# First shift tiles as one-column products, and the repeated row of c from products with the identity

## The chip, the cores and the metric

One core of one Trainium2 chip runs the whole program. The time is the device time of one execution in microseconds (us), and the number that is compared is the median over runs.

## The reference, cut to what matters

The program computes two deep blocks over 256 positions of width 1024. The change touches only what stands at the very beginning: the modulation of the first feed-forward layer.

```python
c_act = jax.nn.silu(c)                       # c: one row of 1024
mod = c_act @ w_ada[l] + b_ada[l]            # nine segments of 1024
sh1, sc1, g1, sh2, sc2, g2, sh3, sc3, g3 = jnp.split(mod, N_MOD, axis=-1)
x = x + 0.5 * g1 * swiglu(modulate(x, sh1, sc1), ffn1_gate[l], ffn1_up[l], ffn1_down[l])
...
modulate(x, shift, scale) = rms_norm(x) * (1 + scale) + shift
```

So before the first gate product there must be: silu of c, the scale and the shift of layer 0 (each 1024 values from a 1024 x 1024 piece of `w_ada`), and the root mean square of x at each position.

## The kernel before, in words

Everything is held with the 1024 features on 128 partitions in 8 tiles (k = 0 to 7) and the 256 positions along the free axis. Weights come through a ring of 8 slots (`ring`) of 512 KB each, filled by one queue (SP, sync) in the order in which TensorE's program takes them; slot n + 8 waits until chunk n has been used. The other start loads (vectors, constants, x) go over the ACT queue.

A weight chunk has one of three kinds. A "cut" chunk is split by ScalarE (`weight_upper`, L2459) and VectorE (`weight_lower`, L1736) into two halves in fp32r; a product then runs as one pass of 512 columns with the upper and one of 256 with the lower half. An "ada" chunk is used by VectorE alone: L1747 multiplies 128 rows of transposed `w_ada` by `c_rows` (the row silu(c), repeated on all partitions) and sums along the row, which gives one tile (128 values) of the modulation. A "whole" chunk is used by TensorE in plain fp32.

In layer 0 the eight scale tiles and the first four shift tiles (`BY_ROW = 4`) are "ada" chunks. The other four shift tiles come from TensorE: `shift_rows` multiplies the column c (as a weight of one column) with 512 moving columns of `w_ada_row`, two products for each of four chunks; ScalarE copies the resulting row of 512 values to SBUF (L2534), `shift_columns` turns it back into four columns with four products, and VectorE adds the bias (L1788).

TensorE's order at the start is: `hold` (products of the identity with itself into an unused bank, which only fill time), then row chunk 0, the sums of squares of x (`squares_sum`, 16 products with one moving column), `spread` (two products that spread the reciprocal root over partitions), row chunks 1 to 3, `shift_columns`, `hold`, and the first gate tile. VectorE's `normalise` makes for each k the scaled x (L1799) and, after ScalarE has rounded the sum with the shift (`normed_upper`, L2539), the lower half (`normed_lower`, L1807); in between it does the ada chunks that are due. The first gate tile takes k after k as `normed_lower` comes in; everything behind it on TensorE follows without waits.

All products are recorded at one line (L601), so the rows below are told apart by their tiles and shapes. In plain fp32 one product is two records.

Of the kernel before, what the change touches and what calls it, by code (L numbers as in the profile page):

```python
# [12 lines left out]
P = 128  # L13
# [43 lines left out]
BY_ROW = 4  # L57
SHIFTS_AT = 5
ADA_AHEAD = 6
ROW_W = D - BY_ROW * P  # L60
ROW_CHUNKS = KD * ROW_W // CW
ROW_BANK = 8 - ROW_W // 512
LAG = 2
# [94 lines left out]
SHARED = {"root_part": "root", "c_silu": "c_act", "shift_row": "c_act", "shifts": "ada_mod",  # L158
# [77 lines left out]
def program(nc, dram, out, seen, stream):  # L236

    ctx = ExitStack()
    with ctx:
# [231 lines left out]

        def pair_bank(f):
            return (0, 1, 2, 3, 6, 7)[f % 6]
# [46 lines left out]
        ADA_FIRST = [seg * KD + k for k in range(KD) for seg in (1, 0) if seg or k < BY_ROW]  # L520
# [3 lines left out]
        first_row = work[0:1, 0:ROW_W].rearrange("p (b c) -> p b c", c=512)  # L524
# [25 lines left out]
        def _(pe):  # L550
# [14 lines left out]
            def cut(name, i, which="weight_lower"):  # L565

                n = take_chunk(name, i, CW, "cut")
                j = split_no[n] = len(split_no)
                pe.wait_ge(*of(which, j))
                return (w_hi[:, j % SPLITS, :], w_lo[:, n % RING, :]), ("cut_used", j), ("weights_used", n)  # L570

# [223 lines left out]
            def shift_rows(j):  # L795

                w, used = arrived("w_ada_row", j)
                if j == 0:
                    refill(6, 7)
                passes = CW // 512  # L800
                for m in range(passes):
                    i, b = (j, ROW_BANK + m) if ROW_W == D else (passes * j + m, ROW_BANK)
                    mn = mm(bank[0:1, b, :], vec("c", i), w[:, m * 512:(m + 1) * 512], i == 0, i == KD - 1)
                mn.then_inc(*did("shift_row_raw", j, also=[used]))
                readers[6] = readers[7] = [("shift_row", 0)]

            def shift_columns():

                pe.wait_ge(*of("shift_row", 0))
                refill(3)  # L810
                for k in range(BY_ROW, KD):
                    a = (k - BY_ROW) * P
                    mn = mm(bank[:, 3, k:k + 1], work[0:1, a:a + P], ones[0:1, 0:1], True, True)
                mn.then_inc(*did("shift_cols_raw", 0))
                readers[3] = [("shifts", 0)]
# [2404 lines left out]
```

## Time and profile before

| what | value |
| --- | --- |
| median of 3 runs (lowest, highest) | 2163.93 us (2163.75, 2165.28) |
| time of the profiled execution | 2162.36 us |
| span of the profiled execution | 2160.6 us |
| PE busy | 2103.5 us (97%) |
| DVE busy | 1521.8 us (70%) |
| ACT busy | 1167.8 us (54%) |
| first feed-forward product starts | 39.99 us |
| its 16th record (the end of the first gate tile) hands over at | 43.23 us |

The span runs from the first to the last instruction, and the execution's own time is 1.8 us more. PE is TensorE, DVE VectorE, ACT ScalarE, POOL GpSimd, SP the sync engine, whose queue loads the weights. Busy time counts records that overlap once.

### The profile page before, as it was taken

The page shows a single profiled execution, that of the slowest core. Times are in us where ns is not written, and L with a number is a line of the kernel's source. Part 1 is how long each engine was busy: PE and PEld are TensorE (multiplying, and loading weights), DVE is VectorE, ACT ScalarE, POOL GpSimd, SP SyncE. Part 2 cuts the span into 40 slices and gives each one's busy share as a digit, 9 for nine tenths or more (in the row PEclk, how much of TensorE's full clock was granted, in tenths as well). Part 3 has the DMA queues.
Part 4 walks back from the last instruction along what each step waited for, and adds up shares of the span by engine and source line. Part 5 has one row for each costly group of instructions (what it writes and reads, how often), then busy time and mean ns, then how long its engine had stood idle before and what let it go on. Part 6 is the DMA issues. An engine that isn't in the chain of part 4 may idle for free.

```text
span 2160.6 us, 40536 instructions
## 1 busy us (share of the span) xinstructions
PE 2103.5 (97%) x16664; PEld 1888.2 (87%) x16664; DVE 1521.8 (70%) x2114; ACT 1167.8 (54%) x2030; POOL 374.2 (17%) x357
## 2 busy tenths in 40 slices
PE   8999999999999999999999999999999988999998
PEld 5888988988888889899888998988888877898887
DVE  6897757788779878577776687477558544647754
ACT  4564556665546545576655575465446632446542
POOL 0131021211102110221011002120132640123001
PEclk9999999999999999999999999999999999999999
DMA  8987772567668777725565544345543400434552
GB/s 306 352 302 271 271 253 99 176 237 265 251 217 303 292 257 270 251 94 181 211 216 205 195 168 155 135 172 192 180 163 136 166 4 4 149 129 162 189 185 98
DMA packets 116679, 424.66 MB, mean 197 GB/s; under 512 B 12944, under 2 KB 14736, under 8 KB 115600
## 3 DMA queue, kind: packets, MB, share of 16 engines
q1 hardware_dynamic: 112896, 409.52, 53.7%
q10 hardware_dynamic: 3600, 12.55, 1.6%
q8 instruction: 133, 2.18, 0.4%
q14 instruction: 50, 0.41, 0.1%
HBM read 418.35 MB, written 3.67 MB: 195 GB/s over the span
## 4 chain that ended last, share of the span: by engine, by line
PE 82%; DVE 7%; issue 5%; ACT 4%; POOL 1%; DMA 1%; SPq 0%; POOLq 0%; ACTq 0%; DVEq 0%
PE banks L601 81%; DVE weight_lower L1736 2%; POOL heap L3030 1%; ACT weight_upper L2459 1%; ACT xn_t L2637 1%; DMA weight_ring<-w_ada_row_dram 0%; PE banks L1556 0%; ACT heap L2637 0%; PE banks L1135 0%; DMA weight_ring<-w_in_dram 0%; DVE nmax L1883 0%; DVE heap L2076 0%; ACT heap L2651 0%; DVE xn_t L1954 0%; DVE xn_t L1957 0%
## 5 line engine op out<-in xcount | busy, mean ns | idle before, releaser
L1736 DVE TENSOR_TENSOR weight_lower<-weight_ring,weight_upper 128x1024 fp32r<-128x1024 f32 x580 | 743.2, 1288 | 265.9 <-ACT weight_upper L2459 263.9
L601 PE MATMUL banks<-xn_halves,weight_upper 128*128 128x512 f32 (+1 forms) x3680 | 808.3, 342 | 0.9 <-DVE xn_halves L2059 0.7
L2459 ACT ACTIVATE weight_upper<-weight_ring 128x1024 fp32r<-128x1024 f32 x580 | 608.4, 1054 | 299.9 <-PE banks L601 195.0
L601 PEld LDWEIGHTS banks<-xn_halves,weight_upper 128*128 128x128 f32 x3680 | 611.9, 188 | 67.7 <-issue 1.4
L601 PE MATMUL banks<-xn_halves,weight_lower 128*128 128x256 f32 x2832 | 519.4, 281 | 2.8 <-DVE weight_lower L1736 1.6
L601 PEld LDWEIGHTS banks<-xn_halves,weight_lower 128*128 128x128 f32 x2832 | 431.6, 188 | 30.0 <-DVE weight_lower L1736 2.4
L601 PE MATMUL banks<-hidden,weight_upper 128*128 128x512 f32 x1216 | 308.8, 393 | 0.6 <-DVE heap L2201 0.6
L3030 POOL TENSOR_TENSOR heap<-heap 128x256 f32<-128x256 f32 x120 | 121.7, 1018 | 873.8 <-ACT heap L2754 587.5
L601 PEld LDWEIGHTS banks<-hidden,weight_upper 128*128 128x128 f32 x1216 | 217.0, 189 | 37.7 <-DVE heap L2201 0.7
L1747 DVE CUSTOM_DVE_ANT_0 weight_ring<-weight_ring,c_rows,vecs 128x1024 f32<-128x1024 f32 x140 | 184.4, 1321 | 19.3 <-DMA weight_ring<-w_ada_dram 18.8
L601 PEld LDWEIGHTS banks<-hidden,weight_lower 128*128 128x128 f32 x1216 | 169.2, 190 | 14.0
L601 PE MATMUL banks<-hidden,weight_lower 128*128 128x256 f32 x1216 | 173.2, 282 | 0.0
L3017 POOL TENSOR_TENSOR heap<-heap 128x256 f32<-128x256 f32 x88 | 76.4, 869 | 479.9 <-ACT heap L2569 479.4
L601 PE MATMUL banks<-heap 64*64 64x64 f32 (+8 forms) x2432 | 120.0, 256 | 16.5 <-issue 5.5
L601 PEld LDWEIGHTS banks<-heap 64*64 64x64 f32 (+4 forms) x2432 | 102.8, 144 | 31.4 <-issue 20.8
L601 PE MATMUL banks<-heap,weight_ring 64*64 64x15 f32 (+2 forms) x944 | 107.0, 287 | 0.8 <-DVE heap L2230 0.4
L2560 ACT ACTIVATE heap<-banks 128x512 f32<-128x512 f32 x88 | 52.2, 593 | 94.2 <-PE banks L601 94.2
L601 PEld LDWEIGHTS banks<-heap,weight_ring 64*64 64x64 f32 (+2 forms) x944 | 86.2, 158 | 15.2 <-issue 2.7
L1829 DVE TENSOR_TENSOR heap<-banks,heap 128x512 f32<-128x512 f32 x88 | 60.4, 686 | 30.7 <-ACT heap L2560 30.5
L601 PE MATMUL banks<-weight_ring,heap 128*128 128x128 f32 (+1 forms) x528 | 73.4, 289 | 0.0
L601 PEld LDWEIGHTS banks<-weight_ring,heap 128*128 128x128 f32 x528 | 63.7, 192 | 6.4 <-issue 6.3
L2486 ACT ACTIVATE heap<-x_t 128x256 f32<-128x256 f32 x56 | 22.4, 411 | 84.0 <-DVE x_t L1821 79.4
(311 smaller groups left out, 2415.5 us busy)
## 6 DMA issues: line engine op xcount, KB each, us to landing
weight_ring<-w_ada_dram SPq DMA_DIRECT2D x140, 512.0 KB, 4.6
weight_ring<-ffn_gate_dram SPq DMA_DIRECT2D x88, 512.0 KB, 3.9
weight_ring<-ffn_up_dram SPq DMA_DIRECT2D x88, 512.0 KB, 4.5
weight_ring<-ffn_down_dram SPq DMA_DIRECT2D x88, 512.0 KB, 3.4
weight_ring<-m_w_up_dram SPq DMA_DIRECT2D x64, 512.0 KB, 3.2
weight_ring<-m_w_down_dram SPq DMA_DIRECT2D x64, 512.0 KB, 3.2
weight_ring<-w_in_dram SPq DMA_DIRECT2D x58, 512.0 KB, 4.3
weight_ring<-b_w_rkv_dram SPq DMA_DIRECT2D x24, 512.0 KB, 3.6
```

The costliest lines, as they stand in the source:

```text
L601: return nc.tensor.matmul(o, w, r, start=first, stop=last)
L1736: V.tensor_tensor(w_lo[:, n % RING, :], ring[:, n % RING, :], w_hi[:, j % SPLITS, :].bitcast(F32), ALU.subtract).then_inc(*did("weight_low ...
L1747: V.tensor_tensor_reduce(w, w, c_rows[:, :], half, vec("b_ada", i), ALU.mult, ALU.add, mod[:, i:i + 1]).then_inc(*did("ada_mod", i, also=[ ...
L1829: V.tensor_tensor(gu[:, f % 4], bank[:, b:b + 2, 0:S], gu[:, f % 4], ALU.add).then_inc(*did("gate_up", (s, f)))
L2459: A.activation(w_hi[:, j % SPLITS, :], ring[:, n % RING, :], ACT.Copy).then_inc(*did("weight_upper", j))
L2486: A.activation(sq[:, k, :], X[:, k, :], ACT.Square).then_inc(*did("squares", (n, k)))
L2560: A.activation(gu[:, f % 4], bank[:, b:b + 2, S:2 * S], ACT.Copy).then_inc(*did("gate_up_half", (s, f)))
L2637: A.activation(s_, s_, ACT.Exp, bias=nmax[:, u % 4, j:j + 1], accum_out=den[:, u % 4, j:j + 1]).then_inc(*did("exp", (l, u, j), also=[("ex ...
L3017: G.tensor_tensor(gu[:, f % 4, 0, :], gu[:, f % 4, 0, :], gu[:, f % 4, 1, :], ALU.mult).then_inc(*did("hidden", (s, f)))
L3030: G.tensor_tensor(acc, acc, sum_tile(n, what, f), ALU.add).then_inc(*did("sum_added", (n, what, f)))
```

## The change

It does four things.

1. All eight shift tiles of layer 0 come from TensorE. `first_shift(k)` takes a chunk of `w_ada_shift` (the 1024 x 128 columns of tile k, as eight 128 x 128 blocks), uses the eight blocks as weights and the eight columns of c as one moving column each, and sums in one column of a bank. ScalarE adds the bias in `shift` (new L2541). `shift_rows`, `shift_columns` and the four shift chunks on VectorE go away.
2. `c_rows` is no longer loaded (512 KB). The column form of c (4 KB) and the identity (64 KB) are loaded first on SP's queue, eight products of a column of c, repeated 128 times, with the identity make the repeated row in two banks, and ScalarE's silu reads it from there.
3. The small work on `lam` (two exponential-type functions on ScalarE, four small operations on VectorE) stands before the squares of x, where it stood behind the root.
4. The first gate tile is split: k = 0 to 4, then `first_shift(7)`, then k = 5 to 7. VectorE's lower halves run two tiles behind the scaling for this layer (`lag`), and its weight half for the gate comes at k = 6 (`FIRST_SPLIT`). `hold` is 4 products after the products of c and 2 after each of the first six shift tiles; the `hold` of 20 before the gate tile is gone.

```diff
-        ADA_FIRST = [seg * KD + k for k in range(KD) for seg in (1, 0) if seg or k < BY_ROW]
+        ADA_FIRST = [KD + k for k in range(KD)]
...
-            sp.dma_start(c_rows[:, :], dram["c_rows"]).then_inc(*did("c_rows_in", 0, by=16))
+            sp.dma_start(vec("c", 0, KD), dram["c_columns"]).then_inc(*did("c_in", 0, by=16))
+            sp.dma_start(ident, dram["ident"]).then_inc(*did("ident_in", 0, by=16))
...
-            def shift_rows(j):
-            def shift_columns():
+            def first_shift(k):
+
+                w, used = arrived("w_ada_shift", k)
+                b = shift_bank(k)
+                refill(b)
+                for j in range(KD):
+                    mn = mm(bank[:, b, 0:1], w[:, j * P:(j + 1) * P], vec("c", j), j == 0, j == KD - 1)
+                mn.then_inc(*did("shift_raw", k, also=[used]))
+                readers[b] = [("shifts", k)]
...
-                    project_wide_first(items(0)[0:1], xn_hl, ("normed_lower", norm), ADA_FIRST[-1:])
+                    name, i, done, readers_of, b = items(0)[0]
+                    refill(b)
+                    w, *used = cut_taken(name, i)
+                    held["first_cut"] = len(order)
+                    first_shift(KD - 2)
+                    ada_take(ADA_FIRST[-1:])
+                    pe.wait_ge(*of("weight_lower", 0))
+                    took = w, used, done, readers_of, b
+                    first_tile(took, xn_hl, norm, range(FIRST_SPLIT - 1))
+                    first_shift(KD - 1)
+                    first_tile(took, xn_hl, norm, range(FIRST_SPLIT - 1, KD))
...
+            for k in range(KD):
+                mn = mm(cols(k // 4, P, k % 4 * P), vec("c", k).broadcast_to((P, P)), ident, True, True)
+            mn.then_inc(*did("c_raw", 0))
+            readers[0] = readers[1] = [("c_act", 0)]
+            hold(2, 4)
             pe.wait_ge(*of("consts_in", 0))
             pe.wait_ge(*of("c_silu", 0))
-            hold(2, 8)
-            for k in range(BY_ROW):
-                ada_take(ADA_FIRST[2 * k:2 * k + 2])
+            ada_take(ADA_FIRST[0:1])
+            for k in range(KD - 2):
+                ada_take(ADA_FIRST[k + 1:k + 2])
+                first_shift(k)
+                hold(2, 2)
                 if k == 1:
                     for j in range(KD):
                         squares_sum(0, j, KD)
+                elif k == 2:
                     spread(0)
-                elif k > 1:
-                    hold(2, 4)
-                shift_rows(k)
-            ada_take(ADA_FIRST[2 * BY_ROW:-1])
-            shift_columns()
-            hold(2, 20)
...
+                    if n == 0:
+                        if k == FIRST_SPLIT:
+                            work_ahead(held["first_cut"])
+                        act.wait_ge(*due("shift_raw", k))
+                        A.activation(mods(0, 0, k), bank[:, shift_bank(k), 0:1], ACT.Identity, bias=vec("b_ada", k)).then_inc(
+                            *did("shifts", k))
+                        act.wait_ge(*due("shifts", k))
                     act.wait_ge(*due("scaled", (n, k)))
```

TensorE's program before, from behind the spread to the first gate record. `1x512` is a product of one weight column with 512 moving columns, `consts` alone is a `hold`, `consts,heap` with `128x1` is here `shift_columns`:

```order
L601 MATMUL banks<-weight_ring,vecs 1x512 [waits weights_in_5]
L601 MATMUL banks<-weight_ring,vecs 1x512
L601 MATMUL banks<-consts 128x128 x4
L601 MATMUL banks<-weight_ring,vecs 1x512 [waits weights_in_0]
L601 MATMUL banks<-weight_ring,vecs 1x512
L601 MATMUL banks<-consts 128x128 x4
L601 MATMUL banks<-weight_ring,vecs 1x512 [waits weights_in_3]
L601 MATMUL banks<-weight_ring,vecs 1x512
L601 MATMUL banks<-consts,heap 128x1 [waits c_act]
L601 MATMUL banks<-consts,heap 128x1 x3
L601 MATMUL banks<-consts 128x128 x20
L601 MATMUL banks<-xn_halves,weight_upper 128x512 [waits normed_lower,weight_lower]
```

The same stretch in the changed program. The first row of a shift tile waits for its chunk, and the row `x7` holds its other seven products:

```order
L605 MATMUL banks<-vecs,weight_ring 128x1 [waits shifts,weights_in_0]
L605 MATMUL banks<-vecs,weight_ring 128x1 x7
L605 MATMUL banks<-consts 128x128 x2
L605 MATMUL banks<-vecs,weight_ring 128x1 [waits shifts,weights_in_2]
L605 MATMUL banks<-vecs,weight_ring 128x1 x7
L605 MATMUL banks<-consts 128x128 x2
L605 MATMUL banks<-vecs,weight_ring 128x1 [waits shifts,weights_in_4]
L605 MATMUL banks<-vecs,weight_ring 128x1 x7
L605 MATMUL banks<-consts 128x128 x2
L605 MATMUL banks<-vecs,weight_ring 128x1 [waits shifts,weights_in_6,c_act]
L605 MATMUL banks<-vecs,weight_ring 128x1 x7
L605 MATMUL banks<-xn_halves,weight_upper 128x512 [waits normed_lower,weight_lower]
```

Where there were three pairs of 512-column products, four small ones and 28 holds, there are now four shift tiles of eight one-column products each (k = 3 to 6), with three holds of two between them. The tile k = 7 follows inside the gate tile. Tiles 0 and 1 stand in front of the sums of squares and tile 2 between them and the spread, each with a hold of two.

ScalarE's program before, from the root to the weight half of the gate (`xn_t,mod` is the upper half of one tile of x, `heap<-banks 1x512` the copy of the row):

```order
L2493 ACTIVATE root<-banks,consts 128x2 [waits bank_filled]
L2716 ACT_TABLE_LOAD
L2716 ACTIVATE lam<-lam 128x8 [waits dve_chain]
L2718 ACT_TABLE_LOAD
L2718 ACTIVATE lam<-lam 128x8 [waits lam_exp]
L2539 ACTIVATE xn_halves<-xn_t,mod 128x256 [waits scaled] x4
L2534 ACTIVATE heap<-banks 1x512 [waits bank_filled]
L2539 ACTIVATE xn_halves<-xn_t,mod 128x256 [waits scaled,ada_mod]
L2539 ACTIVATE xn_halves<-xn_t,mod 128x256 [waits scaled]
L2459 ACTIVATE weight_upper<-weight_ring 128x1024 [waits weights_in_7]
```

In the changed program the end of the same stretch reads (`banks,vecs 128x1` is the bias of one shift tile):

```order
L2541 ACTIVATE mod<-banks,vecs 128x1 [waits bank_filled]
L2545 ACTIVATE xn_halves<-xn_t,mod 128x256 [waits scaled,shifts]
L2541 ACTIVATE mod<-banks,vecs 128x1 [waits bank_filled]
L2545 ACTIVATE xn_halves<-xn_t,mod 128x256 [waits scaled,shifts]
L2541 ACTIVATE mod<-banks,vecs 128x1 [waits bank_filled]
L2545 ACTIVATE xn_halves<-xn_t,mod 128x256 [waits scaled,shifts]
L2464 ACTIVATE weight_upper<-weight_ring 128x1024 [waits weights_in_5]
```

The pair stands six times ahead of the weight half of the gate. Each upper half now waits for its own shift tile from TensorE, and the weight half of the gate stands behind the sixth of them. The two rows of `lam` have moved ahead of the squares of x.

## Rows read from the trace of the kernel before

**Rows 1.** The page: the chain that ended last, by engine.

```profile
PE 82%; DVE 7%; issue 5%; ACT 4%; POOL 1%; DMA 1%; SPq 0%; POOLq 0%; ACTq 0%; DVEq 0%
```

**Rows 2.** Chain that ended last, 0 to 90 us: start, us, what.

```profile
12.39 10.50 PE banks L601 x36
...
42.77 47.46 PE banks L601 x266
```

**Rows 3.** PE in order of time: start, us, what, xrecords, [idle before <-releaser].

```profile
7.51 3.78 PE L601 MATMUL banks<-consts 128*128 128x128 f32 x16 [7.51 <-DMA consts<-consts_dram]
12.39 3.57 PE L601 MATMUL banks<-weight_ring,vecs 128*1 128x512 f32 x4 [1.10 <-DMA weight_ring<-w_ada_row_dram]
15.89 6.99 PE L601 MATMUL banks<-consts,heap 128*128 128x1 f32 x32
23.59 1.20 PE L601 MATMUL banks<-consts,root 128*128 128x128 f32 x4 [0.71 <-DVE root L1783]
24.72 3.12 PE L601 MATMUL banks<-weight_ring,vecs 128*1 128x512 f32 x4
...
31.76 1.88 PE L601 MATMUL banks<-weight_ring,vecs 128*1 128x512 f32 x4
...
35.29 4.73 PE L601 MATMUL banks<-consts 128*128 128x128 f32 x40
...
40.80 0.39 PE L601 MATMUL banks<-xn_halves,weight_upper 128*128 128x512 f32 x1
...
41.15 0.39 PE L601 MATMUL banks<-xn_halves,weight_upper 128*128 128x512 f32 x1
...
43.23 2.09 PE L601 MATMUL banks<-xn_halves,weight_upper 128*128 128x512 f32 x8
```

**Rows 4.** ACT in order of time.

```profile
5.51 1.06 ACT L2709 ACTIVATE c_rows<-c_rows 128x1024 f32<-128x1024 f32 x1 [2.08 <-DMA c_rows<-c_rows_dram]
...
11.26 2.56 ACT L2486 ACTIVATE heap<-x_t 128x256 f32<-128x256 f32 x8 [4.60 <-DMA x_t<-x_dram]
...
23.20 1.28 ACT L2716 ACT_TABLE_LOAD   x1
...
26.01 0.21 ACT L2718 ACTIVATE lam<-lam 128x8 f32<-128x8 f32 x1
...
36.41 1.04 ACT L2459 ACTIVATE weight_upper<-weight_ring 128x1024 fp32r<-128x1024 f32 x1
38.44 0.51 ACT L2539 ACTIVATE xn_halves<-xn_t,mod 128x256 fp32r<-128x256 f32 x1 [0.99 <-DVE xn_t L1799]
```

**Rows 5.** DVE in order of time.

```profile
24.83 0.87 DVE L1799 SCALAR_TENSOR_TENSOR xn_t<-x_t,mod,banks 128x256 f32<-128x256 f32 x2 [0.84 <-PE banks L601]
...
33.41 1.28 DVE L1747 CUSTOM_DVE_ANT_0 weight_ring<-weight_ring,c_rows,vecs 128x1024 f32<-128x1024 f32 x1
...
38.72 1.22 DVE L1736 TENSOR_TENSOR weight_lower<-weight_ring,weight_upper 128x1024 fp32r<-128x1024 f32 x1
```

**Rows 6.** Windows of all engines: at the end PEclk, DMA share, GB/s.

```profile
10.00:15.00 5.00, 3.90 (x11) 1.34 (x9) 2.53 (x4) 3.72 (x9) 0.00 (x0) 1.00 1.03 415
```

**Rows 7.** PE in order of time, one-column products at 164 us.

```profile
164.01 0.95 PE L601 MATMUL banks<-consts,heap 128*128 128x1 f32 x8
```

**Rows 8.** PE in order of time, around 1658 us.

```profile
1655.80 1.84 PE L601 MATMUL banks<-consts,heap 128*128 128x2 f32 x16
...
1658.35 0.28 PE L601 MATMUL banks<-shifted_lower,weight_upper 128*128 128x256 f32 x1
...
1659.25 0.41 PE L601 MATMUL banks<-shifted_lower,weight_upper 128*128 128x256 f32 x1
```

**Rows 9.** Windows of PE there: us, busy (xrecords), PEclk, DMA share, GB/s.

```profile
1658.00:1659.00 1.00, 1.00 (x9) 0.91 0.65 262
1659.00:1660.00 1.00, 1.00 (x7) 0.50 0.00 0
...
1662.00:1663.00 1.00, 1.00 (x10) 0.88 0.00 0
```

More of the change, by code:

```diff
@@ L157 @@
 FILLED = ("square_sums", "rstd", "head_sums", "head_spread", "chunk_used")
-SHARED = {"root_part": "root", "c_silu": "c_act", "shift_row": "c_act", "shifts": "ada_mod",
+SHARED = {"root_part": "root", "c_silu": "c_act",
           "x_last": "x_first",
@@ L793, in project_wide, with first_tile, project_wide_first @@
                 readers[b] = readers_of
-            def shift_rows(j):
[L797 to L805, printed above, removed]
-            def shift_columns():
[L809 to L815, printed above, removed]
-            def project_wide_first(items, x, ready, after=()):
+            def first_shift(k):
[6 more added lines that the diff above has]
+                readers[b] = [("shifts", k)]
+            def first_tile(took, x, norm, ks):
+                w, used, done, readers_of, b = took
+                for k in ks:
+                    pe.wait_ge(*of("normed_lower", (norm, k)))
+                    mm_upper(b, w, k, x, k, k == 0)
+                    mn = mm_lower(b, w, k, x, k, k == KD - 1)
+                    if k == KD - 1:
+                        mn.then_inc(*did(*done, also=used))
+                        readers[b] = readers_of
+            def project_wide_first(items, x, ready):
                 for *_, b in items:
@@ L821, in project_wide_first @@
                 took = [(*cut(name, i), done, readers_of, b) for name, i, done, readers_of, b in items]
-                held.setdefault("first_cut", len(order))
-                ada_take(after)
                 for k in range(KD):
@@ L2718, in _ @@
             A.activation(lam[:, 2, :], lam[:, 2, :], ACT.Ln, bias=1.0).then_inc(*did("lam_ln", 0))
+            act.wait_ge(*due("x_in", 0))
+            squares(0, None)
+            root_of(0)
             for l in range(DEPTH):
@@ L3140, in laid_out @@
     d = {}
-    d["c_rows"] = np.broadcast_to(a["c"][0], (P, D))
+    d["c_columns"] = columns(a["c"].reshape(-1))
+    d["ident"] = CONSTS["ident"]
     d["x"] = a["x"][0].T.reshape(KD, P, S).transpose(1, 0, 2)
-    d["consts"] = np.concatenate([CONSTS[k] for k in CONSTS if k not in ATTN + DELTA], 1)
+    d["consts"] = np.concatenate([CONSTS[k] for k in CONSTS if k not in ATTN + DELTA + ["ident"]], 1)
     d["delta_consts"] = np.concatenate([CONSTS[k] for k in DELTA], 1)
```

80 lines of the change are left out of this document (33 added, 47 removed).

## Prediction

> **What bounds the kernel now.** I read the page first: TensorE is 82% of the chain that ended last [rows 1], so what is gained or lost at the start is kept to the end. The chain over the first 90 us [rows 2] shows where the start ends: TensorE is on it from 12.39, when the first row chunk has landed, then there is a relay with VectorE and ScalarE, and from 42.77 on TensorE alone for 47 us. The mark that counts is therefore the end of the first gate tile, where TensorE goes on with the next chunk: 43.23 [rows 3].
>
> Then I read TensorE in order of time for its pace. At 7.51, 16 records of the identity with itself take 3.78 us, 236 ns each; at 35.29 the same form takes 4.73 us for 40, 118 ns each [rows 3]. The first is 1.2 GHz, the second 2.4 GHz. The PEclk column says 1.00 even where the pace is the slow one [rows 6], so at the start of the trace it must be read from durations. The four 512-column records take 3.57 us at 12.39, 3.12 us at 24.72 and 1.88 us at 31.76: the clock rises at the last of the four at 24.72, near 27.2, after 3.6 us of wide products without a break. The 32 one-column records at 15.89 take 6.99 us, 218 ns each: TensorE issued them without a gap for 7 us, and the clock did not rise.
>
> The opposite case stands later. Eight one-column records at 164.01 take 0.95 us, 119 ns each [rows 7]: that is their price at the high clock. But at 1655.80, 16 narrow records (two columns) take 1.84 us, and 1.2 us later, in the middle of dense products, the clock falls: 256-column records go from 0.28 to 0.41 us [rows 8], and PEclk, which does show this one, is 0.50 in between: its means of 0.91 and 0.88 at the edges put the fall at 1658.8 and the rise at 1662.2 [rows 9]. The records at 1658.35 and 1659.25 stand on either side. Less than 2 us of narrow products among wide ones were enough to lose the clock.
>
> **The change part by part.** A shift tile is 8 products, so 16 records. Its cost is bounded by 16 x 119 ns = 1.9 us [rows 7] and 16 x 218 ns = 3.5 us [rows 3]. A hold of two is 4 records: 0.47 us or 0.94 us. In the new order a hold of two is the only wide work between shift tiles, while around 1655.80 there were full trains of wide products on both sides and the clock still fell. I take the slow price for all eight: the slow row is the nearer one, since it too has nothing wide around it.
>
> The Trainium skill (TensorE: Matmul & The Clock Gate, Part 1 and "Loop structure matters more than you think") explains the low clock by idleness and says that matmuls kept back to back stay warm. By that rule the eight tiles would run at 1.9 us each, which is the first rival below. The trace disagrees twice: 7 us of gapless one-column records without a rise, and a fall after gapless narrow ones.
>
> The start: c and the identity are 68 KB in place of 512 KB, and 68 KB of constants move off the ACT queue. The first shift chunk is third in the ring like the first row chunk, which was in use at 12.39 [rows 3]; 512 KB fewer (both queues) at 415 GB/s [rows 6] are 1.3 us: 11.1 us. The products for c begin at about 3.6 us, between 3.0 (the fastest a small load could be there) and 5.5 (when the 512 KB had landed [rows 4]); 16 records are 3.8 us, silu 1.06, so silu(c) is ready near 8.6 and hidden under the load. The two functions of `lam` are now ahead of the squares on ScalarE, 3.0 us with their table loads (23.20 to 26.22 [rows 4]): 8.6 + 3.0 = 11.6, so the squares end at 14.2 instead of 13.8. Hidden too: TensorE does not reach them before 20. The price of `lam` would be 0.4 us if the cover were gone. On VectorE four chunks of 1.3 us [rows 5] go away, of which two were behind the root: 2.7 us less. That is hidden now, because VectorE will wait for TensorE.
>
> TensorE's own queue from 11.1 us, at the low clock:
>
> - shift 0, hold, shift 1, hold: 2 x (3.5 + 0.94) = 8.9, to 20.0
> - sums of squares, unchanged 7.0: to 27.0
> - shift 2 and hold 4.4, spread 1.2: to 32.6. The root (0.5 us on ScalarE and VectorE) is hidden under shift 2
> - shifts 3, 4, 5 with holds: 13.3, to 45.9
> - shift 6: 3.5, to 49.4
> - gate tile k = 0 to 4: 0.35 us each at the high clock (40.80 to 41.15 [rows 3]), 0.70 at half of it: 3.5, to 52.9
> - shift 7: 3.5, to 56.4
> - gate tile k = 5 to 7: 2.1, to 58.5
>
> Is anything else later? VectorE starts at 32.6 instead of 24.8. The weight half of the gate stands on ScalarE behind the upper half of k = 5, thus behind shift 5 (45.0): 0.2 + 0.5 + 1.04 [rows 4], then 1.2 on VectorE [rows 5]: 47.9, under shift 6. The chunk of shift 6 can be loaded only once shift 2 is done (30.5), 15 us ahead of its use. Behind shift 7 ScalarE and VectorE need 0.2 + 0.5 + 0.5 = 1.2 us, to 57.6, while k = 5 and 6 last until 57.8. So TensorE is the bound throughout: 58.5 against 43.23, 15.3 us late.
>
> Before, the high clock was there at 43.23; now it is still to rise. Dense work begins at 56.4. The row of 1658.8 shows 3.4 us at 1.2 GHz under dense work, and at the start 8.4 us (7.51 to 15.89) with one gap of 1.1 us did not bring the rise. Thus it comes between 59.8 and 64.8; what lies behind 58.5 costs half its length: 0.7 to 3.1 us. I take 1.3, near the short end, because at 24.72 it also took 3.6. In the other direction, the products for c and the hold are 5.7 us of wide work and may lift the clock for the first shift tile: 0 to 1.6 us back, I take 0.5.
>
> Sum: 15.3 + 1.3 - 0.5 = 16.1 us. The profiled execution had 2162.36 us, 1.8 over its span; with the sum 2178.5. The median of the runs is 1.6 higher, 2163.93, so the forecast is 2180.0 us, 0.74% slower. Later stages give nothing back, TensorE is full there.
>
> **The rivals.**
>
> *One-column products run at the high clock* (the other sign). For it: 164.01, and the holds put between. Then shift 0 and 1 end with holds at 16.0, the squares at 19.9, shift 2 and hold 22.3, spread 22.8, against 24.8 before. From there VectorE is the bound: 16 operations at 0.40 (two take 0.87 with their overlap), 4 chunks at 1.33 (1.28 and a read), one weight half 1.2 [rows 5] are 12.9 us, with 1.6 us of waiting for shift 7 about 37.3, the tile ends at 37.7: 5.5 us earlier, 2158.4. It decides if the clock rises before the first shift tile and stays; against it stand the two stretches named.
>
> *The clock is held until the squares and falls there.* The 5.7 us of wide work lift it, holds keep it over two shift tiles, the 16 narrow products in a row lose it. Squares end at 19.9, then the slow queue: shift 2, hold, spread 5.6, three tiles with holds 13.3, shift 6, five gate steps, shift 7, three gate steps 12.6, the end at 51.4; 8.2 + 1.3 = 9.5 later, 2173.4.
>
> *The clock rises and falls several times*, lifted by a hold and lost in the next tile: the time lies between those two, 2159 to 2173. Against it: even 3.8 us of wide records at 7.51 did not raise it [rows 3].
>
> *A load is late*, as the ring gives a slot back only after a slow shift tile. The slots have 15 us of slack; at most 1 to 2 us on top.
>
> **How the numbers follow.** Low clock throughout 0.86, clock until the squares 0.05, high clock 0.05, up and down 0.04. The range must reach over the unknowns of the likeliest case: 2.4 us of the rise, 1.6 us of the lift at the start, 0.5 us of loads on either side, and the next rival: 2173 to 2184. A measurement of this kernel tells 0.2% (4.3 us) from no change. Faster by more than that is only most of the second case, 0.05; within 0.2%: 0.04; slower: 0.91.
>
> **What would show it.** Right: one-column records of the shift tiles at about 218 ns, spread near 32 us, the gate tile split around a shift tile of 3.5 us, the second gate chunk begun near 58 us, VectorE waiting for TensorE several us in all between 30 and 50, and 256-column records still at 0.4 us for a few us after 58. Wrong: one-column records at 119 ns, or a first gate record before 40. A first shift tile much later than 11 us would move everything by as much, and mean that the load of 512 KB was not what the start waited for.

## The result and the profile after

| kernel | median | lowest to highest | runs |
| --- | --- | --- | --- |
| before | 2164.61 us | 2163.75 to 2168.66 | 4 |
| changed | 2189.44 us | 2188.07 to 2190.70 | 4 |

The ratio is 1.0111, with a 95% interval of 1.0097 to 1.0124: the change makes the kernel 24.8 us slower. The forecast was slower too, but 2180.0 us with a range of 2173 to 2184; the time lies 9.4 us above the forecast and 5.4 us above the range. The profiled execution of the changed kernel took 2188.07 us (span 2186.2 us), 25.7 us more than that of before. PE is busy 2129.2 us (97%).

Its chain that ended last, first by engine from the page, then the view of 0 to 110 us (start, us, what), against [rows 1, 2]:

```profile
PE 83%; DVE 6%; issue 4%; ACT 4%; POOL 1%; DMA 1%; SPq 0%; POOLq 0%; ACTq 0%; DVEq 0%
```

```profile
2.58 10.26 DMA weight_ring<-w_ada_shift_dram
12.84 0.14 issue
12.98 97.13 PE banks L605 x484
```

From 12.98 on there is TensorE alone. No relay with the other engines is left, so TensorE's pace at the start is paid in full. TensorE in order of time, against [rows 3]:

```profile
4.41 3.65 PE L605 MATMUL banks<-consts,vecs 128*128 128x128 f32 x16 [4.41 <-DMA consts<-ident_dram]
7.90 1.06 PE L605 MATMUL banks<-consts 128*128 128x128 f32 x8
12.98 3.54 PE L605 MATMUL banks<-vecs,weight_ring 128*128 128x1 f32 x16 [4.02 <-DMA weight_ring<-w_ada_shift_dram]
16.38 1.20 PE L605 MATMUL banks<-consts 128*128 128x128 f32 x4
17.38 3.41 PE L605 MATMUL banks<-vecs,weight_ring 128*128 128x1 f32 x16
...
21.64 6.83 PE L605 MATMUL banks<-consts,heap 128*128 128x1 f32 x32
...
33.59 3.41 PE L605 MATMUL banks<-vecs,weight_ring 128*128 128x1 f32 x16
...
49.66 0.77 PE L605 MATMUL banks<-xn_halves,weight_upper 128*128 128x512 f32 x1
...
53.01 3.41 PE L605 MATMUL banks<-vecs,weight_ring 128*128 128x1 f32 x16
...
58.63 3.62 PE L605 MATMUL banks<-xn_halves,weight_upper 128*128 128x512 f32 x8
```

The eight hold records at 7.90 take 132 ns each, so the clock had just risen. Every one-column tile behind the idle time of 4.02 us takes 3.41 to 3.55 us for 16 records, the slow price. The first gate tile ends at 58.63, against 43.23 before. The clock column shows the fall and the rise (windows of PE: us, busy, PEclk, DMA share, GB/s):

```profile
11.00:12.00 1.00, 0.00 (x0) 0.62 1.03 422
12.00:13.00 1.00, 0.02 (x1) 0.50 1.02 418
61.00:62.00 1.00, 1.00 (x3) 0.50 0.95 385
62.00:63.00 1.00, 1.00 (x8) 0.78 0.93 373
```

The 1.2 GHz level thus lasts from 11.2 to 62.4 us. That is the forecast's mechanism, but it does not explain the whole loss. To find the rest I compare the starts of one kind of instruction, ScalarE's loads of function tables, of which each trace has 35 in the same order. The table gives, in us, how much later than in the profiled execution of before five of them start, for all kernels of this document (worked out from the traces). Where a stretch of low clock is named below, it is read from PEclk in windows of 1 us, and its length is twice the sum of what is missing to 1.00.

```
mark (its start before)          5th 52.53  7th 279.65  9th 302.77  33rd 1836.09  35th 1962.57
changed                            +17.1      +18.7       +22.7       +25.0         +25.7
changed, second profile            +16.6      +17.8       +22.0       +25.2         +25.2
before, second profile              -1.8       -0.4        +0.0        +3.5          +3.8
e1  shift tiles 128 wide            -2.8       -1.5        +3.5        +9.0          +9.7
e2  c's row by identity alone       -3.6       -2.1        -1.0        +5.7          +5.9
e3  no holds                        +7.5       +8.7        +8.6       +15.3         +15.3
e4  e1 and sums 128 wide            -4.4       -4.1        +2.8        +7.5          +8.3
e5  longer hold                    +11.3      +12.1       +11.6       +15.4         +16.2
e6  before, 40 more holds           +8.7       +8.4       +12.4       +17.8         +18.3
e7  e4 without holds                -6.6       -6.9        -7.5        -8.5          -8.4
e8  before, sums 128 wide           -2.8       -2.7        -2.4        +1.0          +1.2
e9  e1 without holds                -0.8       +2.4        +2.0        +4.2          +4.3
e10 shift tiles alone              +16.5      +17.7       +24.4       +27.6         +27.8
```

The changed kernel loses 17.1 us at the start (16.1 were forecast), 1.6 by the 7th mark, 4.0 between the 7th and the 9th, and 3.0 behind it. So there were two questions for the chip: is the low clock made by the one column, and what are the later 8.6 us?

### The profile page after: what moved, and what is told of

Read it like the earlier page. It is cut to its first block, busy times and chain, and to the rows that moved or that the text cites. A ratio compares the mean times of both kernels' runs of the same rounds, so it can differ in the third digit from the quotient of the medians.

```text
span 2186.2 us, 40704 instructions
## 1 busy us (share of the span) xinstructions
PE 2129.2 (97%) x16744; PEld 1920.8 (88%) x16744; DVE 1512.1 (69%) x2105; ACT 1168.7 (53%) x2037; POOL 371.9 (17%) x357
## 4 chain that ended last, share of the span: by engine, by line
PE 83%; DVE 6%; issue 4%; ACT 4%; POOL 1%; DMA 1%; SPq 0%; POOLq 0%; ACTq 0%; DVEq 0%
PE banks L605 82%; DVE weight_lower L1749 1%; POOL heap L3037 1%; ACT weight_upper L2464 1%; ACT xn_t L2643 1%; DMA weight_ring<-w_ada_shift_dram 0%; PE banks L1569 0%; ACT heap L2643 0%; PE banks L1144 0%; DVE nmax L1888 0%; ACT heap L2657 0%; DVE heap L2081 0%; DVE xn_t L1959 0%; ACT spare L2961 0%; DVE xn_t L1962 0%
## 5 line engine op out<-in xcount | busy, mean ns | idle before, releaser
L1760 DVE CUSTOM_DVE_ANT_0 weight_ring<-weight_ring,c_rows,vecs 128x1024 f32<-128x1024 f32 x136 | 176.4, 1301 | 22.5 <-DMA weight_ring<-w_ada_dram 21.8
L605 PE MATMUL banks<-heap,weight_ring 64*64 64x15 f32 (+2 forms) x944 | 112.9, 294 | 3.1 <-issue 2.6
```

The lines of the kernel that those rows point to most:

```text
L605: return nc.tensor.matmul(o, w, r, start=first, stop=last)
L1760: V.tensor_tensor_reduce(w, w, c_rows[:, :], half, vec("b_ada", i), ALU.mult, ALU.add, mod[:, i:i + 1]).then_inc(*did("ada_mod", i, also=[ ...
```

## The experiments

All medians of before in this part come from the same chip as the kernel beside them. A product in plain fp32 is two records; a `hold(2, n)` is n products, so 2n records.

**Width and holds.** Experiment e1 makes the shift tiles 128 columns wide (c's column repeated; the same sum stands in each column). Experiment e3 takes away the holds between the tiles.

```diff
 e1
-  mn = mm(bank[:, b, 0:1], w[:, j * P:(j + 1) * P], vec("c", j), j == 0, j == KD - 1)
+  mn = mm(bank[:, b, 0:P], w[:, j * P:(j + 1) * P], vec("c", j).broadcast_to((P, P)), j == 0, j == KD - 1)
 e3
   first_shift(k)
-  hold(2, 2)
```

> The changed kernel, but each product of a shift tile moves the column of c repeated 128 times in place of one column: the same number of products and weight loads, 128 times the moving columns; the reader takes column 0. Theory (narrow products lose TensorE's clock): the clock comes up during the first two tiles, a tile costs 1.9 us in place of 3.4, the first gate tile ends near 42 us in place of 58.6 and needs no new rise, so 15 to 19 us less than the changed kernel: 2170 to 2174 us. Rival (the cost is the number of products, each bound by its weight load, and the clock has other reasons): no gain, or up to 2 us slower (236 in place of 218 ns a record), 2189 to 2192 us.

> The changed kernel without the six holds of two between the shift tiles. Theory (the clock is low there in any case): the holds are pure cost, 6 x 0.95 us = 5.7 us less than the changed kernel, 2183 to 2184.5 us, and the records of shift tiles stay at 213 to 218 ns. Rival (the holds help the clock): no gain, or slower.

Measured: e1 2172.56 us against 2166.85, ratio 1.0035 (1.002 to 1.005); e3 2177.20 us, ratio 1.0055 (1.0038 to 1.0072). First TensorE of e1 in order of time, then e3's:

```profile
10.93 2.02 PE L605 MATMUL banks<-vecs,weight_ring 128*128 128x128 f32 x16 [1.62 <-DMA weight_ring<-w_ada_shift_dram]
...
15.73 3.94 PE L605 MATMUL banks<-consts,heap 128*128 128x1 f32 x32
19.52 3.76 PE L605 MATMUL banks<-vecs,weight_ring 128*128 128x128 f32 x16
...
27.47 1.95 PE L605 MATMUL banks<-vecs,weight_ring 128*128 128x128 f32 x16
```

```profile
10.87 6.30 PE L605 MATMUL banks<-vecs,weight_ring 128*128 128x1 f32 x32 [1.77 <-DMA weight_ring<-w_ada_shift_dram]
17.03 6.96 PE L605 MATMUL banks<-consts,heap 128*128 128x1 f32 x32
...
28.26 13.65 PE L605 MATMUL banks<-vecs,weight_ring 128*128 128x1 f32 x64
41.78 0.77 PE L605 MATMUL banks<-xn_halves,weight_upper 128*128 128x512 f32 x1
...
45.12 2.14 PE L605 MATMUL banks<-vecs,weight_ring 128*128 128x1 f32 x16
```

In both the first chunk came early, behind an idle time of under 2 us. The wide tile then costs 1.95 to 2.05 us at the high clock, the narrow one 3.2 to 3.5 us. A wide record costs 122 ns at the high clock and a narrow one 119 [rows 7]: with its stationary operand changed for each product, the 128 columns are nearly free. At the start of e1 only the sums, still one column wide, lose the clock (it is low from 18.9 to 25.7 us, so the tile at 19.52 is wide and slow). In e3 the clock falls at 11.6 us within the first tile and stays low: 80 one-column records stand there in a row without a gap and, behind the spread, another 64. It is back at 45.7, after the five gate steps at 41.78, and low once more from 49.2 to 52.6. e3 is 12.2 us faster than the changed kernel, twice the 5.7 us that were expected: the start gives 9.6 us of it (the six holds are 24 records of about 250 ns, 6 us, and the clock is back by 46 instead of 62), and a piece of 4 us at the 9th mark is missing, which is taken up below.

e9, described further down, is e3 with 128 columns in the shift tiles and no other difference. Its first two tiles and its tiles 3 to 6:

```profile
11.11 5.44 PE L605 MATMUL banks<-vecs,weight_ring 128*128 128x128 f32 x32 [1.87 <-DMA weight_ring<-w_ada_shift_dram]
...
25.24 7.51 PE L605 MATMUL banks<-vecs,weight_ring 128*128 128x128 f32 x64
```

Its clock falls at 12.0 us within the first tile too, but the wide tiles bring it back at 15.4 and, after the sums, at 25.7. It is low for 13.7 us before 40 us, and e3's for 34.1, and the first gate tile ends at 42.39 instead of 49.19.

**Hold the clock through the wait.** Experiment e5 fills the idle time ahead of the first shift tile in the changed kernel.

```diff
-            hold(2, 4)
+            hold(2, 16)
             pe.wait_ge(*of("consts_in", 0))
```

> The changed kernel with 16 instead of 4 rounds of two hold products behind the products of c, so that TensorE has work in most of the 4.0 us for which it waited for w_ada_shift before the first shift tile; nothing else is altered. Theory: the clock fell in that kernel at 11.2 us, in this idle time, but the one-column products behind it are not enough to keep it, so it falls again within the shift tiles and squares: the first gate tile still ends later than 50 us (58.6 us in the changed kernel), and the time is 2180 to 2190 us. The rival says that a clock that is high on entry stays high through the one-column products, as the narrow products of 7.8 to 11.2 us had it: then the squares' two blocks of 32 take 3.8 us instead of 6.9, the shift tiles 1.9 instead of 3.5, the first gate tile ends near 42 us and the time is 2170 us or less. For the later pause: with 24 more instructions ahead of it, the pause of 2.6 us with the reason issue at about 307 us, in the stage of 64x15 products, is gone or stands elsewhere by the theory that their number places it, and is unchanged by the rival that the waits of data set it.

Measured: 2182.23 us against 2166.04, ratio 1.0068 (1.0053 to 1.0083), 7.2 us under the changed kernel. TensorE in order of time:

```profile
7.99 4.00 PE L605 MATMUL banks<-consts 128*128 128x128 f32 x32
11.83 1.92 PE L605 MATMUL banks<-vecs,weight_ring 128*128 128x1 f32 x16
13.61 0.69 PE L605 MATMUL banks<-consts 128*128 128x128 f32 x4
14.29 2.63 PE L605 MATMUL banks<-vecs,weight_ring 128*128 128x1 f32 x16
16.79 1.20 PE L605 MATMUL banks<-consts 128*128 128x128 f32 x4
17.78 6.83 PE L605 MATMUL banks<-consts,heap 128*128 128x1 f32 x32
```

This case leaves idle time out. The clock is high on entry, there is no gap, and it falls at 15.4 us, inside the second one-column tile. (The rival in the expectation calls the work of 7.8 to 11.2 us narrow; it was eight hold records of 128 columns and then idle time.) So the idle time of 4.02 us only brings the fall forward; without it the one-column work makes it. The forecast's lift for the first tile (0.5 us, at most 1.6) exists here and not in the changed kernel, whose clock fell while it waited. The pause that is dealt with below is gone too.

**One half at a time.** Experiment e2 is the kernel before with c's row made by products with the identity (part 2 of the change alone, with its shorter hold). Experiment e10 is the changed kernel with the 512 KB load and the hold of 8 back (the shift tiles, with parts 3 and 4 of the change).

```diff
 e2, e10 the other way round
-  sp.dma_start(c_rows[:, :], dram["c_rows"]).then_inc(*did("c_rows_in", 0, by=16))
+  sp.dma_start(vec("c", 0, KD), dram["c_columns"]).then_inc(*did("c_in", 0, by=16))
+  sp.dma_start(ident, dram["ident"]).then_inc(*did("ident_in", 0, by=16))
...
+  for k in range(KD):
+      mn = mm(cols(k // 4, P, k % 4 * P), vec("c", k).broadcast_to((P, P)), ident, True, True)
```

> The kernel before with only the second part of the change: c and the identity are loaded (68 KB), eight products make the repeated row, and the shift stays with the 512-column products. If the 512 KB load is what the start waits for, the first row chunk is used 1.3 us earlier and the time is about 1 us less than before. If the start is bound by what is behind it (TensorE's squares at the low clock, then VectorE), or the small loads are no earlier, the difference is under 0.5 us. If the products for c and the hold behind them bring the clock up early, the sums of squares run at 119 in place of 218 ns and up to 3 us are gained.

> The changed kernel with c's repeated row loaded as 512 KB again, as in the kernel before, so that only the one-column shift tiles remain of the change (its other half alone was measured at 2166.5 us, ratio 1.0003). Theory: the loss is the shift tiles' and this kernel has all of it: the clock stays low from the start until the gate tiles, which begin when their tiles are split, so the first gate tile ends between 57 and 62 us and the time is 2184 to 2194 us. If the loss came from both halves together, by the idle time that the early products leave ahead of the first shift tile, this kernel ends well under 2184 us.

Measured: e2 2166.49 us against 2166.85, ratio 1.0003 (0.9993 to 1.0012); e10 2188.05 us against 2165.55, ratio 1.0098 (1.0080 to 1.0116). So part 2 costs nothing that is clear of noise, and the loss lies in the rest. Parts 3 and 4 have no run of their own, but e1, which keeps both and only widens the shift tiles, is 2.8 us ahead of before at the 5th mark: at the start the loss is that of the one-column tiles. In e2 the first row chunk is in use at 11.06 instead of 12.39 [rows 3], 1.3 us earlier as worked out, and by the 5th mark its profiled execution is 1.8 us ahead even of the second profile of before, but the measured time does not show it. e10's first shift tile starts at 12.88 and its gate tile ends at 58.55, within 0.1 us of the changed kernel. Its clock column must not be read there: it shows 1.00 at 20 us, where the 16 records at 17.30 take 3.41 us. As in [rows 6], it stands at 1.00 until the first step that the trace has.

**The pause near 290 us.** Between the 7th and the 9th mark the changed kernel loses 4.0 us. The cause in its trace is a pause of TensorE that ends with "issue": it waited for no data. Here are that row of the changed kernel and its clock (windows of PE):

```profile
307.58 3.86 PE L605 MATMUL banks<-heap,weight_ring 64*64 64x15 f32 x18 [2.62 <-issue]
```

```profile
307.00:308.00 1.00, 0.41 (x11) 1.00 0.09 37
308.00:309.00 1.00, 1.00 (x3) 0.60 0.06 25
309.00:310.00 1.00, 1.00 (x4) 0.50 0.07 20
311.00:312.00 1.00, 1.00 (x4) 0.69 0.00 0
```

The pause is 2.62 us, and behind it the clock is low for 3.4 us. The kernel before has 0.34 us in this stage, 63 records ahead of its end (the last eight are 128x256 products with the same tiles):

```profile
285.93 2.93 PE L601 MATMUL banks<-heap,weight_ring 64*64 64x15 f32 x63 [0.34 <-issue]
```

e1 and e4 have the long pause too, at the same 18 records before the end of the stage, though their start is fast; e3 has none. What these share is the number of TensorE's records: 16664 before, 16744 in the changed kernel, e1 and e4, 16720 in e3. Hence experiment e6, the kernel before with 40 hold products, 80 records, more and nothing else (its expectation calls the records products and places them ahead of the products of c, while they stand ahead of the first gate tile), and a second profile of each of the two kernels.

```diff
-            hold(2, 20)
+            hold(2, 60)
```

> The kernel before with 60 instead of 20 rounds of two hold products ahead of the first product of c, 80 products of TensorE more and no other edit: the products of c and all that follows start later. At the low clock 80 products of two columns add at most 8.5 us (106 ns each), of which what the load of c's row already takes is hidden. Theory: the number of instructions ahead also places a pause in the stage of 64x15 products; it is 0.34 us in before and 2.6 to 3.6 us in three kernels whose start has more instructions, and a stretch of low clock stands beside it. Then this kernel loses, beyond what its first gate tile ends later, 2 to 4 us between 280 and 303 us. The rival, that this pause is made by what the change does to the data, expects nothing there: the loss at 303 us equals the loss at 53 us within 0.5 us.

> The kernel before, unchanged, profiled once more. If the low-clock stretches after 60 us belong to the program, this trace has the same single one as the profiled execution of before (1658 to 1663 us, 3.4 us at the low clock) and a span within 0.5 us of its 2160.6. If they vary from execution to execution, the low stretches stand at other places or in another number and the span is several microseconds away (the plain runs of before reach from 2160.3 to 2169.8). In both cases the pause of TensorE in the stage of 64x15 products near 290 us that ends with the reason issue stays 0.34 us, since the program is the same; if that pause moves or grows here too, its cause is not the number of instructions ahead of it.

> The changed kernel, unchanged, profiled once more. If the pause of 2.6 us with the reason issue at about 307 us belongs to the program, it is here again at the same place, between 2 and 4 us long; if it comes from one execution it is gone. The 51 us at the low clock at the start should be the same within 2 us, and the first gate tile end at 58 to 59 us. The later low stretches should stand partly elsewhere, as in the two traces of the kernel before; the time 2186 to 2192 us.

Measured: e6 2177.50 us against 2166.04, ratio 1.0049 (1.0034 to 1.0064); b1 2166.16 us; b2 2187.58 us. The row of e6, then that of b1, then that of b2, then e10's (TensorE in order of time):

```profile
297.45 3.75 PE L601 MATMUL banks<-heap,weight_ring 64*64 64x15 f32 x15 [2.75 <-issue]
```

```profile
285.97 2.92 PE L601 MATMUL banks<-heap,weight_ring 64*64 64x15 f32 x63 [0.73 <-issue]
```

```profile
306.87 3.74 PE L605 MATMUL banks<-heap,weight_ring 64*64 64x15 f32 x18 [2.83 <-issue]
```

```profile
308.69 3.99 PE L604 MATMUL banks<-heap,weight_ring 64*64 64x15 f32 x9 [2.92 <-issue]
```

e6 has nothing of the change and has the pause: it loses 8.7 us by the start and 3.9 us more between the 7th and the 9th mark. Counting TensorE's records from the start to the pause gives 1974 in the changed kernel, b2, e1 and e4, 1977 in e6 and 1975 in e10. The pause is tied to a place in TensorE's own instruction stream, in six traces among the short 64x15 products.

The same shows late in the program, where short 64x64 products stand. All fourteen traces have such a wait at record 13068 to 13073 (0.45 to 1.89 us) and again at 13320 to 13324 (0.73 to 1.63 us), although up to 104 records more stand ahead of it in one kernel than in another. The second of the two in before and in e5 (TensorE in order of time):

```profile
1781.11 0.57 PE L601 MATMUL banks<-heap 64*64 64x64 f32 x23 [1.33 <-issue]
```

```profile
1790.85 1.40 PE L605 MATMUL banks<-spare,heap 64*64 64x64 f32 x65 [1.63 <-issue]
```

What TensorE waits for can be read from the DMA queues. The page of the changed kernel has one of the kind "instruction" (packets, MB, share):

```profile
q8 instruction: 134, 2.20, 0.4%
```

Its packets are 16 KB each. There are 133 for the 16664 records of before and 134 for the 16744 of the changed kernel, one for about 125 records, and the places above are 125 (1849 and 1974) or 251 records apart. The table has the packet next to the pause, in us (worked out from the packets in the traces):

```
                 record  TensorE stops  packet            TensorE goes on
changed          1974    304.96         305.39 to 306.36  307.58
changed, second  1974    304.04         304.62 to 305.51  306.87
e1               1974    284.79         286.17 to 287.05  288.42
e4               1974    282.12         282.58 to 283.50  284.93
e6               1977    294.71         295.02 to 296.03  297.45
e10              1975    305.76         306.25 to 307.25  308.69
before           1849    285.59         283.59 to 284.51  285.93
before, second   1849    285.23         283.58 to 284.59  285.97
e8               1849    282.93         281.35 to 282.36  283.57
e5               1974    no stop        295.43 to 296.39  (record at 297.79)
```

TensorE goes on 1.2 to 1.4 us behind the end of a packet each time. It is so everywhere: the fourteen traces have 71 waits of at least 0.8 us that end with "issue", and each ends 1.2 to 1.7 us behind the end of such a packet, though one comes only every 16 us in the mean. By these times TensorE waits there for the next 16 KB of its own instructions. In the six long pauses the packet starts only after TensorE has stopped; in before and e8 it starts 1.6 to 2.0 us ahead of the stop. In e5, with 104 records more than before, it ended 1.4 us before the record was due, and nothing waits. In e3, e7 and e9, with 56 records more, record 1974 lies behind the stage, in 128x512 products, and in before, e2 and e8 in 128x256 products, and the packet is there in time. What makes the packet start late in six traces is not shown.

**The rest, and the way to a faster kernel.** Experiment e4 is e1 with the sums of squares 128 columns wide as well (each column holds the same sum; one sum of the joined norms stays at one column); e7 is e4 without the holds between the tiles; e9 is e1 without them, its sums narrow; e8 is the kernel before with only the sums wide.

```diff
 e4, e7, e8 (and the later sums alike)
-  mn = mm(bank[:, 4 + t, 0:1], src[:, k, t * P:(t + 1) * P], ones[:, 0:1],
+  mn = mm(bank[:, 4 + t, 0:P], src[:, k, t * P:(t + 1) * P], ones[:, 0:P],
```

> The first experiment, and in addition every sum of squares in the program (start, norms of all layers, the memory, the latents) moves 128 columns of ones in place of one. Theory: the clock no longer falls at the start once it is up, and the later falls that stand beside sums of squares (at 277 us in the trace of the changed kernel) go away: the gate tile ends near 39 us and the time is 2156 to 2164 us, below the kernel before. Falls beside the narrow products that are left (15 columns wide near 308 and 895 us, 64 x 64 tiles near 1840 us) can stay. Rival for the later 8.6 us (not the clock, but loads that come late because the ring is shifted): the later part keeps its extra time, whatever the sums look like.

> The kernel with products of 128 columns in the shift tiles and in all sums of squares, without the hold products between the shift tiles. Theory: the wide products keep the high clock by themselves, so leaving out the holds costs nothing and takes away their own time (two rounds after each shift tile); the first gate tile ends at 37.5 to 38.8 us (38.8 with the holds), the pause near 290 us is gone as in the narrow kernel without holds, and the time is 2164 to 2169 us, 3 to 5 us under the same kernel with the holds. If the holds keep the clock, it falls between the shift tiles here: low stretches before 40 us, the first gate tile past 42 us, and 2172 us or more.

> The kernel before with 128 columns instead of one in all sums of squares, the widening that the fastest kernel so far also has; nothing of the change. It tells what of that kernel's 2161.2 us the widening alone gives. Theory: the sums at 15.9 us take 3.8 us at the high clock instead of 6.99 at the low one if the clock is high by then, as in the second trace of the kernel before, and the clock does not fall beside them: the first gate tile ends 1 to 4 us earlier and the time is 2161 to 2165 us, so most of what was gained belongs to the widening. The rival, that the early load of c is what gains, has this kernel at 2165 to 2168 us, as before.

> The changed kernel with 128 columns in the shift tiles and no hold products between them, but one column in the sums of squares as it was. Theory: the shift tiles ahead run at the high clock, the 32 narrow sums lose it again, and a stretch of 5 to 9 us at the low clock follows before the later wide tiles bring it back, as it did with the holds (18 to 26 us there); the first gate tile ends at 38 to 41 us and, without the pause near 290 us, the time is 2164 to 2169 us, 3 to 6 us over the kernel that has wide sums too. If the time is 2161 to 2163, the width of the sums was worth nothing.

Measured, each against before on its chip: e4 2171.15 us, ratio 1.0034 (1.0022 to 1.0046); e7 2161.24 us, 0.9976 (0.9964 to 0.9989); e8 2164.52 us, 0.9993 (0.9982 to 1.0004); e9 2166.51 us, 0.9993 (0.9981 to 1.0006). e4 misses its forecast of 2156 to 2164 us, e7 is faster than its 2164 to 2169. e7 is the only kernel that beats before. TensorE in order of time there:

```profile
10.95 2.02 PE L605 MATMUL banks<-vecs,weight_ring 128*128 128x128 f32 x16 [1.62 <-DMA weight_ring<-w_ada_shift_dram]
13.42 2.05 PE L605 MATMUL banks<-vecs,weight_ring 128*128 128x128 f32 x16 [0.45 <-DMA weight_ring<-w_ada_shift_dram]
15.31 3.73 PE L605 MATMUL banks<-consts,heap 128*128 128x128 f32 x32
...
21.11 5.82 PE L605 MATMUL banks<-vecs,weight_ring 128*128 128x128 f32 x48
...
30.90 0.50 PE L605 MATMUL banks<-xn_halves,weight_upper 128*128 128x512 f32 x1 [1.45 <-DVE weight_lower L1749]
...
36.62 2.10 PE L605 MATMUL banks<-xn_halves,weight_upper 128*128 128x512 f32 x8
```

Its first gate tile ends at 36.62, 6.6 us ahead of before, and its only low stretch before the last products is 3.4 us at 1807. TensorE now waits 1.45 us for VectorE at 30.90: the bound of the start has passed to the other engines. e9 lacks only the wide sums, and its gate tile ends at 42.39. Of its three low stretches before 40 us, though, only the second (18.8 to 25.7) begins in the sums; the first begins in the first wide tile behind 1.87 us of idle time, and the third (35.9) behind a wait of 2.32 us for VectorE. The interval of its ratio touches that of e7, so what the wide sums add to the wide tiles is not settled. e4 differs from e7 only in the holds and loses 9.9 us to it by the medians. Their profiled executions are 16.7 us apart by the marks, since that of e7 (2154.14 us) was its fastest: 2.2 us at the start, 0.6 up to the 7th mark, 7.5 at the place of the pause, where the clock of e4 is also low for 10.2 us, and 6.4 behind it, with 13.6 us of low clock in e4 between 1819 and 1848 against 3.4 in e7. In e4 the clock had also fallen at 10.8 us, at the end of a wait of 2.22 us for the first chunk, and the wide tile brought it back at 14.2. e8 says that wide sums alone are not the gain. Its interval touches that of e7, so the share of the early load and the shift tiles in e7's 4.8 us is likely, not certain.

## Why the prediction was right in direction and too low in size

- *The slow price for all eight tiles* was right to the record: 213 to 222 ns each, 3.41 to 3.55 us a tile. The one column is the cause: e1, with the same order and the same holds, against the changed kernel, and e9 against e3, without holds, have the high clock for most of the start where only the width differs, and e5 loses it without idle time.
- *The first shift tile at 11.1 us*: 12.98. It was mis-sized by 1.9 us. With the same loads the first chunk was in use between 10.9 and 11.1 us in e1, e2, e3, e4, e7 and e9, but at 12.56 in the second profile of the changed kernel; e10, with 512 KB more, had it at 12.88. Why both profiles of the changed kernel are the late ones stays open. That the gate tile still ended at 58.63 for 58.5 is luck: most terms behind it (tiles with holds, sums, spread) were 0.1 to 0.5 us shorter than they had been rounded to, 1.75 us in sum.
- *The lift at the start*, -0.5: nothing. The products of c and the hold did raise the clock (132 ns a record at 7.90), and 4.02 us of waiting for the load lost it.
- *The rise after the gate tile*, 1.3: it came at 62.4, inside the 59.8 to 64.8 given, and costs 17.1 - 15.4 = 1.7 us by the 5th mark. (The 3.6 us that the forecast leaned on would have given 0.7, not 1.3.) The start in all is 17.1 for 16.1.
- *VectorE waits for TensorE*: it did, 4.80 us in front of its first scaling at 33.84 and 5.80 us in front of the lower half at 57.29. No other engine came into the sum.
- *"Later stages give nothing back, TensorE is full there"* is the step that failed: it put everything behind the start at nothing, and 8.6 us were lost there. The change also adds 80 records to TensorE's stream, and that puts a wait of 2.6 us for the next 16 KB of instructions and a low clock of 3.4 us, together 4.0 us, into a stage 250 us later. e6 shows 3.9 us there with added hold records alone. The forecast had no term for where in the program a count of instructions falls.
- *"The median of the runs is 1.6 higher"* is a small part: with a fourth run the median of before is 2164.61 instead of 2163.93, which is 0.7 of the 9.4 us. The rest, 8.7, is 1.0 at the start, 4.0 at the pause and 3.7 behind or between them (4.6 by the two profiled executions), and the cause of this last piece stays open. It may be luck: between the start and the last products the profiled execution of before has a single low stretch of 3.4 us, at 1658, but b1, the same kernel, has 17.1 us in four (at 258, 1658, 1818 and 1835), and the two profiles of the changed kernel have 23.9 and 20.5 us. b1 ends 3.8 us later than the first profile, although its start was 1.8 us faster, because the clock rose at the start of the sums instead of at 27.2, as its row shows. Against b1 the changed kernel's 21.9 us come out as 18.9 at the start, 3.6 at the pause, and -0.6 for all the rest.

```profile
16.20 3.87 PE L601 MATMUL banks<-consts,heap 128*128 128x1 f32 x32
```

- *The rival with the high clock* was not what happened, but its sum is nearly that of e7: 37.7 for the gate tile and 2158.4 us forecast; 36.6 and 2161.24 measured. What it lacked was the condition, which e7 meets by other means, with wide products and without the holds.

The rule of the Trainium skill that was weighed (TensorE: Matmul & The Clock Gate, Part 1 and "Loop structure matters more than you think": back-to-back matmuls stay warm) fails here on a third row: e5's 16 one-column records at 14.29 have no idle time ahead of them and the clock falls in them. The fall at 11.2 us in the changed kernel, in an idle time of 4.02 us, does agree with its account of idleness.

What stays open is what makes the instruction packet start late in six traces, and what places the low stretches at 1802 to 1865 us, which all traces but before's first profile have in some length.

## What to carry to other kernels

One-column products in a row cost TensorE its clock, even without a gap. If the stationary operand changes for each product anyway, make the moving operand 128 columns wide by repeating it: a record then costs 122 instead of 119 ns at the high clock, against 213 to 222 ns at the low one, which otherwise reaches into the work behind. The holds tried here between narrow tiles, 4 records after 16, did not repair it and cost 1 us each. A wait that ends with "issue" should be laid beside the packets of the instruction queue before a data wait is looked for. Before a forecast is built on one profile, profile the same kernel twice; here two executions of before differ by 3.8 us with their low stretches at different places, nearly the 0.2% that was to be told apart.

## What was not expected of the hardware

- TensorE can run out of its own instructions. Pauses of 2.6 to 3.6 us sat behind the same record of its stream (1974 to 1977) in six traces of five kernels, each ended 1.2 to 1.4 us behind a 16 KB packet of the instruction queue. 80 hold records added to the kernel before, 250 us earlier, were enough to bring one into short products (0.34 and 0.73 us in two executions of before, 2.75 us in e6).
- With the same queue of loads the time of the first 512 KB chunk in use varied from 10.9 to 13.0 us, more than the 1.3 us that 512 KB less on the queue were worth in e2.
